# Scans, a sum of squares and the squares of heads in three mixers, put behind what the next product waits for

## The chip, the cores and the metric

The kernel runs on one core of a Trainium2 chip. The metric is the device time of one execution in microseconds (us), lower is better. Before the change the median of three runs is 1278.88 us (1277.93 to 1278.93).

## The reference, cut to what matters

Four transformer layers in a row work on one sequence of 256 rows of width 1024, all in float32. Each layer is a mixer and a gated feed-forward net. The mixers are: (1) dilated attention beside a state-space model; (2) a gated linear recurrence (RG-LRU); (3) latent attention (MLA) of 8 heads beside attention over 256 memory rows of 4 heads; (4) grouped-query attention of 8 heads on 2 key heads beside memory attention. The change touches mixers 2, 3 and 4.

```python
# mixer 2, after two gates r and i of the convolved input xc
a = exp(-8 * gate_r * softplus(-lam))
h[t] = a[t] * h[t-1] + sqrt(1 - a[t]**2) * gate_i[t] * xc[t]   # a scan along the rows
y = (h * gelu(z_right)) @ w_out                                # needs h of 1024 channels
# mixers 3 and 4, for each head of 128 channels
q = rmsnorm(q) * gain ; k = rmsnorm(k) * gain                  # mean of squares over the head
p = softmax(q @ k.T * scale) ; out = p @ v
```

## The kernel before, in words

**Products.** The rows lie in two tiles of 128. A weight matrix comes in chunks of 128 x 2048 floats (1 MB) by DMA into three RAW buffers (`weights`, L2473; SP waits for VectorE to be done with a buffer). For precision each chunk is split in a high part WH, by a copy on ScalarE (L1059, some 1.9 us), and a rest WL, by a subtraction on VectorE (L1655, some 2.3 us); activations are split in the same way (YAh by ScalarE, YAl by VectorE). Every product is then three matmuls: high by high, high by rest and rest by high (L451 to L453). `feed(c)` on ScalarE and on VectorE (L1061, L1657) splits the chunk three places after c, when its buffer is free. Transposes are matmuls by an identity matrix (L457).

**Order.** There is no planner: for each of the five engines one function issues a list of instructions written out by hand, and semaphores tie the lists together. Each engine works its own list strictly in order, so an instruction that waits holds all behind it. `fill` functions put other work between the steps of an attention, by head number h.

**Mixer 2.** The 1024 channels are eight tiles, worked as four pairs n = 0 to 3 ("heads" here). VectorE's `gates_scan` (L2095) multiplies (L2101) and scans (L2103) a pair, `gates_out` (L2105) multiplies by the gelu branch GT, ScalarE's `gates_out` (L1428) copies it to YAh, and VectorE's `gates_lo` (L2112) makes YAl (L1671). The product with w_out (`wide_mm`, L532, called with od_out) waits before each of its four chunks for the YAl of one pair (`out_ready`, L892). Ahead of it TensorE multiplies od2 and od3, whose results make GT; behind the first chunk it transposes the last half of them.

**Mixers 3 and 4.** `attention_ahead` exists for TensorE (L714), ScalarE (L1517) and VectorE (L2213). On TensorE a step h is: products of head h+2 (L723; waits for the exponentials of head h), transposes of the exponentials of head h, fill(h), pv of head h-1 (L747; waits for VectorE's copy of that head's transposes). ScalarE: exponentials of head h (L1523; wait for the maximum), fill(h). VectorE: maximum `top` of head h+2 (L2216), copy of the transposes of head h (L2238), fill(h).

Within these steps the last heads are still normalised. In mixer 3 query heads n1 (in PSUM banks 6 and 7) and key heads nk1 (banks 4 and 5) are squared by ScalarE into ZD and ZA, summed by `head_sum` (L1789, instruction L1792) on VectorE, turned to 1/sqrt by two small instructions on GpSimd (`rsqrt`, L2346: L2348 and L2350), scaled out of PSUM by `scaled_out` (L2203, instruction L2208), transposed by TensorE's `gain_turn` (L771) into banks 4 and 5, and copied with their gain by ScalarE's `gain_turn` (L1191, called qt1 and kt1 at h = 3 and 5 of L1530). `pvfree2` (L983) lets the first pv go only when n1 has left banks 6 and 7. The transposes of n1 (L979) wait for the scaled_out of nk1, since they write its banks.

In mixer 4 the memory queries g3 go the same way: ScalarE squares them head by head in `fill3` (L1629) with `head_squares` (L1174, instruction L1095, eight squares that each also give their sum), GpSimd makes the factors, VectorE scales them in its fill at h = 3 (`scaled`, L1782, instruction L1787), TensorE transposes them at h = 4 (L1036). `all_squares` (L1183, instruction L1185) is the other form, used elsewhere: one square over all 1024 elements and no sums, with a `head_sum` on VectorE behind it.

Of the kernel before, what the change touches and what calls it, by code (L numbers as in the profile page):

```python
# [198 lines left out]
def numbered(names):  # L199

    return {n: i + 1 for i, n in enumerate(names.split())}
# [11 lines left out]
class Tally:  # L213
# [5 lines left out]
    def up(self):  # L219
# [15 lines left out]
    zq pe zk mem1 n0 nk0 zm qp memk1 n1 nk1 row5 row6 g0 g2 g1 g3 row7"""  # L235
RSTD = numbered(NAMED_RSTD)
HSQ = counted(("memk0", 1), ("zq", 2), ("pe", 2), ("zk", 2), ("n0", 1), ("nk0", 1), ("zm", 1), ("qp", 1), ("memk1", 1),
              ("n1", 1), ("nk1", 1), ("g0", 8), ("g2", 4), ("g1", 8), ("g3", 8))
NZ = counted(*((n, 2) for n in "memk0 zq kp zk n0 nk0 zm qp memk1 n1 nk1 g0 g2 g1 g3".split()))
ZEV = counted(*((n, 2) for n in "za zb zc vt0 z2 vt1 g0 g2 g1 g3".split()))  # L240
GT = counted(("memk0", 2), ("qt0", 2), ("kt0", 2), ("qmt", 2), ("qpt", 2), ("memk1", 2), ("qt1", 2), ("kt1", 2),
             ("g0", 2), ("g2", 1), ("g1", 2), ("g3", 2))
HSUM = numbered("memk0 n0 nk0 zm qp memk1 n1 nk1")
SO = dict(memk0=8, zq=20, zk=22, zm=26, pe=24, memk1=8, qp=42, n0=34, nk0=8, n1=34, nk1=8, g3=26, g2=20, g0=8, g1=34)


def program(nc, A, PLAN, NCH):
# [10 lines left out]
    with top:  # L258
# [137 lines left out]
        JK2 = JK[:, :].rearrange("p (a b) -> p a b", a=2)  # L396
# [52 lines left out]
        def pe(e):  # L449
# [525 lines left out]
                    e.wait_ge(S.gout, GT["kt1"] + 2)  # L975

            def fill2(h):
                if h == 2:
                    gain_turn(ZD, "n1", (4, 5), lambda jp: e.wait_ge(S.nz, NZ["nk1"] + 2))  # L979
                elif h == 4:  # L980
                    gain_turn(ZA, "nk1", (4, 5), lambda jp: e.wait_ge(S.gout, GT["qt1"] + jp + 1))
# [73 lines left out]
        def act(e):  # L1055
# [37 lines left out]
            def squares(out, src, n, total):  # L1093

                return e.activation(out, src, ACT.Square, scale=n ** -0.5, accum_out=total)  # L1095

            def row_squares(ed):
                for t in range(2):
                    if t:
                        e.wait_ge(S.rowsq, 2 * ed + 1)  # L1100
                    squares(JK[:, :], X[:, t, :], 1024, st[:, 2 + t:3 + t]).then_inc(S.rowsq, 1)

            def post_squares(ed, t):
# [403 lines left out]
            def head_norm(name, src, nh=4, d=128, z=None):  # L1507
                e.wait_ge(S.z, ZEV[z] + 2)
                head_squares(name, src, nh, d)
# [119 lines left out]
            def fill3(h):  # L1629
                if h == 1:  # L1630
                    z_evac("g3", PLAN["gqa3"][1], (4, 5), Zg[3], scaled=True)
                elif h == 2:
                    gain_turn("g1", lambda j: QTg[:, 4 + j:6 + j, :], gqg[:, 1:2], (4, 5))
                    e.wait_ge(S.hsq, HSQ["g1"] + 8)
                    head_norm("g3", two(Zg[3]), 4, 128, "g3")
                elif h == 5:
                    gain_turn("g3", lambda j: QMg[:, j:j + 2, :], gqg[:, 0:1], (4, 5))
                elif h == 7:
                    feed(PLAN["gqa3"][1])
# [10 lines left out]
        def dve(e):  # L1650
# [138 lines left out]
            def head_sum(name, sq, d):  # L1789
                n = 1024 // d  # L1790
                e.wait_ge(S.hsq, HSQ[name] + 1)
                e.tensor_reduce(st[:, SO[name]:SO[name] + n], sq.rearrange("p a (h d) -> p (a h) d", d=d), AX.X, ADD).then_inc(S.hsum, 1)  # L1792
# [302 lines left out]
            def gates_scan(ns):  # L2095
                flat = lambda a, hs: a[:, hs, :].rearrange("p a b -> p (a b)")
                for n in ns:
                    hs = slice(2 * n, 2 * n + 2)
                    e.wait_ge(S.b3, n // 2 + 1)
                    e.wait_ge(S.b4, n // 2 + 1)  # L2100
                    e.tensor_tensor(TI[:, hs, :], TI[:, hs, :], HS[:, hs, :], MUL).then_inc(S.dv, dv.up())  # L2101
                    e.wait_ge(S.dv, dv.n)
                    e.tensor_tensor_scan(flat(HS, hs), flat(TR, hs), flat(TI, hs), 0.0, MUL, ADD).then_inc(S.dv, dv.up())  # L2103
# [8 lines left out]
            def gates_lo(ns):  # L2112
                for n in ns:
                    hs = slice(2 * n, 2 * n + 2)
                    e.wait_ge(S.b9, n + 1)
                    rest(YAl[:, hs, :], HS[:, hs, :], YAh[:, hs, :]).then_inc(S.b10, 1)
# [30 lines left out]
            feed(PLAN["od2"][0])  # L2147
            gates_scan((0, 1))
            feed(PLAN["od2"][1])
            gates_scan((2, 3))  # L2150
            gates_out((0, 1))
            gates_lo((0, 1))
            feed(PLAN["od3"][0])
            feed(PLAN["od3"][1])
            wide_mm(PLAN["od_out"], 3, last_heads)
# [132 lines left out]

            def fill2(h):
                if h == 0:  # L2290
                    head_sum("nk1", ZA[:, :, :], 128)
                    scaled_out("n1", ZD, (6, 7))
                elif h == 1:
                    scaled_out("nk1", ZA, (4, 5))
                    feed(PLAN["mem11"][1])
                elif h == 3:
                    feed(PLAN["qb1"][0])
                elif h == 7:
                    feed(PLAN["kvb1"][0])
# [30 lines left out]
            def fill3(h):  # L2330
                if h == 0:
                    feed(PLAN["gqa1"][1])
                elif h == 1:
                    feed(PLAN["gqa3"][0])
                elif h == 3:
                    scaled("g3", two(Zg[3]), 4, 128)
                elif h == 7:
                    feed(PLAN["gqa3"][1])
# [210 lines left out]
```

## Time and profile before

| | us |
|---|---|
| median of three runs (lowest, highest) | 1278.88 (1277.93, 1278.93) |
| the profiled execution's own time | 1277.36 |
| its span, first to last instruction | 1275.6 |
| TensorE busy (share) | 1247.0 (98%) |
| VectorE busy | 815.3 (64%) |
| ScalarE busy | 669.7 (52%) |
| GpSimd busy | 91.3 (7%) |
| weights read | 214.5 MB, 169 GB/s over the span |
| granted TensorE clock, mean | 0.998 |

"Busy" of TensorE counts matmuls whose ends are modelled, so that they overlap a little; gaps between them are what is to be read. PE is TensorE, DVE VectorE, ACT ScalarE, POOL GpSimd. In the views in order of time, a row gives start, duration, engine, line, instruction, output<-input with its size, how many of them are merged, and in brackets how long the engine stood idle before it and who released it.

### The profile page before, as it was taken

The page shows a single profiled execution, that of the slowest core. Times are in us where ns is not written, and L with a number is a line of the kernel's source. Part 1 is how long each engine was busy: PE and PEld are TensorE (multiplying, and loading weights), DVE is VectorE, ACT ScalarE, POOL GpSimd, SP SyncE. Part 2 cuts the span into 40 slices and gives each one's busy share as a digit, 9 for nine tenths or more (in the row PEclk, how much of TensorE's full clock was granted, in tenths as well). Part 3 has the DMA queues.
Part 4 walks back from the last instruction along what each step waited for, and adds up shares of the span by engine and source line. Part 5 has one row for each costly group of instructions (what it writes and reads, how often), then busy time and mean ns, then how long its engine had stood idle before and what let it go on. Part 6 is the DMA issues. An engine that isn't in the chain of part 4 may idle for free.

```text
span 1275.6 us, 15785 instructions
## 1 busy us (share of the span) xinstructions
PE 1247.0 (98%) x6366; PEld 1031.6 (81%) x6366; DVE 815.3 (64%) x1048; ACT 669.7 (52%) x975; POOL 91.3 (7%) x113
## 2 busy tenths in 40 slices
PE   6999999999999999999999999999999999999998
PEld 4877888888887888888888888888888888888886
DVE  7986766654787765564687656565546784665552
ACT  7666544433788554443587635444336653544431
POOL 2410100000110000000123100000000300000000
PEclk9999999999999999999999999999999999999999
DMA  7224465545644565545555224555455323555551
GB/s 298 100 84 143 171 212 184 193 171 198 215 165 165 182 208 188 192 172 198 171 198 192 73 75 161 212 180 198 166 197 177 132 100 132 198 178 185 195 173 62
DMA packets 32392, 216.60 MB, mean 170 GB/s; under 512 B 3888, under 2 KB 4272, under 8 KB 7232
## 3 DMA queue, kind: packets, MB, share of 16 engines
q1 hardware_dynamic: 30240, 210.19, 47.7%
q0 software_dynamic: 1360, 4.78, 1.2%
q8 instruction: 50, 0.82, 0.2%
q10 hardware_dynamic: 720, 0.63, 0.1%
q14 instruction: 22, 0.18, 0.0%
HBM read 214.54 MB, written 1.05 MB: 169 GB/s over the span
## 4 chain that ended last, share of the span: by engine, by line
PE 81%; DVE 10%; ACT 5%; issue 3%; DMA 1%; POOL 1%; SPq 0%; DVEq 0%; ACTq 0%
PE PS L451 22%; PE PS L453 22%; PE PS L452 22%; PE PS L457 4%; DVE WL L1655 3%; PE PS L488 2%; PE PS L491 2%; PE PS L489 2%; PE PS L723 2%; ACT WH L1059 2%; PE PS L747 1%; ACT HTh L1076 1%; DVE YG L1932 1%; DMA RAW<-in_w 1%; DVE st L1792 0%
## 5 line engine op out<-in xcount | busy, mean ns | idle before, releaser
L1655 DVE TENSOR_TENSOR WL<-RAW,WH 128x2048 fp32r<-128x2048 f32 (+2 forms) x200 | 443.9, 2222 | 327.9 <-ACT WH L1059 327.8
L1059 ACT ACTIVATE WH<-RAW 128x2048 fp32r<-128x2048 f32 (+2 forms) x200 | 371.7, 1862 | 381.1 <-PE PS L453 380.1
L451 PE MATMUL PS<-WH,HTh 128*128 128x512 f32 (+1 forms) x848 | 335.0, 395 | 1.9 <-DVE WL L1655 1.9
L453 PE MATMUL PS<-WH,HTl 128*128 128x512 f32 (+1 forms) x848 | 329.0, 388 | 0.0
L452 PE MATMUL PS<-WL,HTh 128*128 128x512 f32 (+1 forms) x848 | 328.4, 387 | 0.0
L451 PEld LDWEIGHTS PS<-WH,HTh 128*128 128x128 f32 x848 | 159.5, 188 | 34.4 <-DVE WL L1655 3.2
L453 PEld LDWEIGHTS PS<-WH,HTl 128*128 128x128 f32 x848 | 159.2, 188 | 33.3
L452 PEld LDWEIGHTS PS<-WL,HTh 128*128 128x128 f32 x848 | 159.6, 188 | 30.5
L451 PE MATMUL PS<-WH,YAh 128*128 128x512 f32 x402 | 158.9, 395 | 2.6 <-DVE YAl L1671 2.2
L453 PE MATMUL PS<-WH,YAl 128*128 128x512 f32 x402 | 156.7, 390 | 0.0
L452 PE MATMUL PS<-WL,YAh 128*128 128x512 f32 x402 | 156.5, 389 | 0.0
L451 PEld LDWEIGHTS PS<-WH,YAh 128*128 128x128 f32 x402 | 75.5, 188 | 18.7 <-issue 4.0
L453 PEld LDWEIGHTS PS<-WH,YAl 128*128 128x128 f32 x402 | 75.4, 188 | 15.9
L452 PEld LDWEIGHTS PS<-WL,YAh 128*128 128x128 f32 x402 | 75.6, 188 | 14.9
L2348 POOL TENSOR_SCALAR st<-st 128x2 f32<-128x2 f32 (+4 forms) x33 | 19.1, 579 | 762.9 <-ACT JK L1095 692.2
L488 PE MATMUL PS<-WH,HTh 128*128 128x512 f32 (+1 forms) x128 | 52.8, 412 | 3.9 <-DVE WL L1655 2.6
L1076 ACT ACTIVATE HTh<-PS,cst 128x128 fp32r<-128x128 f32 (+1 forms) x136 | 39.2, 379 | 26.8 <-PE PS L457 26.8
L491 PE MATMUL PS<-WH,HTl 128*128 128x512 f32 (+1 forms) x128 | 50.5, 395 | 0.0
L489 PE MATMUL PS<-WL,HTh 128*128 128x512 f32 (+1 forms) x128 | 50.5, 394 | 0.0
L1672 DVE SCALAR_TENSOR_TENSOR HTl<-PS,cst,HTh 128x128 fp32r<-128x128 f32 (+1 forms) x136 | 38.9, 351 | 12.5 <-ACT HTh L1076 12.0
L2350 POOL TENSOR_TENSOR st<-st,mh 128x2 f32<-128x2 f32 (+4 forms) x33 | 39.6, 1199 | 2.8
L1076 ACT ACTIVATE YAh<-PS 128x512 fp32r<-128x512 f32 x38 | 21.6, 583 | 25.6 <-PE PS L457 25.6
(364 smaller groups left out, 1488.8 us busy)
## 6 DMA issues: line engine op xcount, KB each, us to landing
RAW<-in_w SPq DMA_DIRECT2D x196, 1024.0 KB, 4.9
BC<-in_rows POOLq DMA_DIRECT2D x4, 512.0 KB, 3.9
YG<-in_mem POOLq DMA_DIRECT2D x4, 512.0 KB, 4.8
X<-in_x SPq DMA_DIRECT2D x2, 512.0 KB, 6.4
RAW<-in_w SPq DMA_DIRECT2D x4, 256.0 KB, 5.8
BC<-in_s SPq DMA_DIRECT2D x1, 512.0 KB, 11.0
BB<-in_s SPq DMA_DIRECT2D x1, 512.0 KB, 11.5
YG<-in_s SPq DMA_DIRECT2D x1, 512.0 KB, 12.3
```

The source lines that it names most:

```text
L451: e.matmul(out, ah, bh, start=start, stop=False)
L452: e.matmul(out, ah, bl, start=False, stop=False)
L453: return e.matmul(out, al, bh, start=False, stop=stop)
L457: return e.transpose(out, src, ident[0:p, 0:p])
L488: e.matmul(out, HTh[:, k, ts], WH[:, c % NW, w], start=k == 0, stop=False)
L489: e.matmul(out, HTh[:, k, ts], WL[:, c % NW, w], start=False, stop=False)
L491: return e.matmul(out, HTl[:, k, ts], WH[:, c % NW, w], start=False, stop=k == 7)
L1059: e.activation(WH[:, c % NW, w], RAW[:, c % NR, w], ACT.Copy).then_inc(S.hi, 1)
L1076: return e.activation(out, src, ACT.Copy, scale=scale)
L1655: e.tensor_tensor(WL[:, c % NW, w], RAW[:, c % NR, w], WH[:, c % NW, w].bitcast(f32), SUB).then_inc(S.lo, 1)
L1672: return e.scalar_tensor_tensor(out, src, gain, hi.bitcast(f32), MUL, SUB)
L2350: e.tensor_tensor(st[:, at:at + n], st[:, at:at + n], mh[:, 0:n], ALU.pow).then_inc(S.rs, 1)
```

## The change

Mixer 2: on VectorE the scans of pairs 2 and 3 come after the gates of pairs 0 and 1 and their YAl. Mixer 3: on VectorE head_sum of nk1 moves from head step 0 to 1, scaled_out of nk1 from step 1 to 2, so that the split of a chunk (`feed(PLAN["mem11"][1])`) now comes before it; on TensorE the transposes of n1 move from step 2 to 3. Mixer 4: the eight squares of g3 with sums become one square without sums, and VectorE sums them in its step 2; the counts of two semaphores follow. ScalarE's last row squares, which write the same scratch, wait for that sum.

```diff
-              ("n1", 1), ("nk1", 1), ("g0", 8), ("g2", 4), ("g1", 8), ("g3", 8))
+              ("n1", 1), ("nk1", 1), ("g0", 8), ("g2", 4), ("g1", 8), ("g3", 1))
...
-HSUM = numbered("memk0 n0 nk0 zm qp memk1 n1 nk1")
+HSUM = numbered("memk0 n0 nk0 zm qp memk1 n1 nk1 g3")
...
 # TensorE
             def fill2(h):
-                if h == 2:
+                if h == 3:
                     gain_turn(ZD, "n1", (4, 5), lambda jp: e.wait_ge(S.nz, NZ["nk1"] + 2))
...
 # ScalarE
                     if t:
                         e.wait_ge(S.rowsq, 2 * ed + 1)
+                    elif ed == 7:
+                        e.wait_ge(S.hsum, HSUM["g3"])
...
                     e.wait_ge(S.hsq, HSQ["g1"] + 8)
-                    head_norm("g3", two(Zg[3]), 4, 128, "g3")
+                    e.wait_ge(S.z, ZEV["g3"] + 2)
+                    all_squares(JK2, Zg[3][:, :, :], 128)
...
 # VectorE
             feed(PLAN["od2"][1])
-            gates_scan((2, 3))
             gates_out((0, 1))
             gates_lo((0, 1))
+            gates_scan((2, 3))
             feed(PLAN["od3"][0])
...
             def fill2(h):
                 if h == 0:
-                    head_sum("nk1", ZA[:, :, :], 128)
                     scaled_out("n1", ZD, (6, 7))
                 elif h == 1:
+                    head_sum("nk1", ZA[:, :, :], 128)
+                    feed(PLAN["mem11"][1])
+                elif h == 2:
                     scaled_out("nk1", ZA, (4, 5))
-                    feed(PLAN["mem11"][1])
...
                     feed(PLAN["gqa3"][0])
+                elif h == 2:
+                    head_sum("g3", JK2, 128)
                 elif h == 3:
```

## Rows read from the trace of the kernel before

**Rows 1.** The page's first part: busy us, share of the span, instructions

```profile
PE 1247.0 (98%) x6366; PEld 1031.6 (81%) x6366; DVE 815.3 (64%) x1048; ACT 669.7 (52%) x975; POOL 91.3 (7%) x113
```

**Rows 2.** Waits of PE over the whole span: total us, times, longest us

```profile
PE PS L451 <- DVE YAl L1671: 2.2, 2, 1.2
...
PE PS L747 <- DVE Z L2208: 1.2, 1, 1.2
```

**Rows 3.** PE in order of time, start of the product with od_out

```profile
413.23 0.47 PE L451 MATMUL PS<-WH,YAh 128*128 128x512 f32 x1 [1.18 <-DVE YAl L1671]
...
418.79 1.04 PE L457 MATMUL PS<-ident,ZN 128*128 128x128 f32 x8
```

**Rows 4.** DVE in order of time, end of mixer 2

```profile
407.18 0.69 DVE L2101 TENSOR_TENSOR TI<-TI,XC 128x512 f32<-128x512 f32 x1
...
411.01 1.29 DVE L2110 TENSOR_TENSOR XC<-XC,GT 128x512 f32<-128x512 f32 x2
412.39 1.29 DVE L1671 TENSOR_TENSOR YAl<-XC,YAh 128x512 fp32r<-128x512 f32 x2
```

**Rows 5.** ACT in order of time, the same stretch

```profile
406.71 1.92 ACT L1059 ACTIVATE WH<-RAW 128x2048 fp32r<-128x2048 f32 x1 [0.93 <-PE PS L453]
```

**Rows 6.** PE in order of time, attention of mixer 3

```profile
716.71 1.13 PE L747 MATMUL PS<-YG,Z 128*128 128x128 f32 x8 [1.19 <-DVE Z L2208]
...
718.54 1.56 PE L457 MATMUL PS<-ident,Z 128*128 128x128 f32 x12
719.94 1.06 PE L747 MATMUL PS<-YG,Z 128*128 128x128 f32 x8
720.83 1.03 PE L723 MATMUL PS<-KM,QMT 128*128 128x256 f32 x4
...
723.40 1.03 PE L723 MATMUL PS<-KM,QMT 128*128 128x256 f32 x4
```

**Rows 7.** DVE in order of time, attention of mixer 3

```profile
712.95 0.69 DVE L2216 TENSOR_REDUCE A2M<-PS 128x2 f32<-128x512 f32 x1 [1.03 <-PE PS L723]
...
714.16 1.21 DVE L1792 TENSOR_REDUCE st<-Z 128x8 f32<-128x1024 f32 x1
...
717.68 1.28 DVE L2208 TENSOR_TENSOR Z<-PS,st 128x512 f32<-128x512 f32 x2
718.87 2.28 DVE L1655 TENSOR_TENSOR WL<-RAW,WH 128x2048 fp32r<-128x2048 f32 x1
```

**Rows 8.** ACT in order of time, the two copies of qt1 in mixer 3

```profile
719.70 1.27 ACT L1076 ACTIVATE QTn<-PS,gq 128x512 f32<-128x512 f32 x2 [1.49 <-PE PS L457]
```

**Rows 9.** A DVE split and POOL, in order of time, before and in the attention

```profile
690.30 2.28 DVE L1655 TENSOR_TENSOR WL<-RAW,WH 128x2048 fp32r<-128x2048 f32 x1
...
690.47 2.21 POOL L2348 TENSOR_SCALAR st<-st 128x8 f32<-128x8 f32 x1 [8.86 <-DVE st L1792]
...
715.46 0.24 POOL L2348 TENSOR_SCALAR st<-st 128x8 f32<-128x8 f32 x1 [8.78 <-DVE st L1792]
715.78 1.67 POOL L2350 TENSOR_TENSOR st<-st,mh 128x8 f32<-128x8 f32 x1
```

**Rows 10.** PE in order of time, attention of mixer 4

```profile
1025.98 1.13 PE L723 MATMUL PS<-KTg,QTg 128*128 128x256 f32 x4 [0.91 <-ACT A3P L1523]
...
1030.52 1.06 PE L747 MATMUL PS<-Zg,A3PT 128*128 128x128 f32 x8
```

**Rows 11.** DVE in order of time, attention of mixer 4

```profile
1026.52 0.68 DVE L2238 COPY A3PT<-PS 128x512 f32<-128x512 f32 x1
...
1028.36 1.28 DVE L1787 TENSOR_TENSOR Zg<-Zg,st 128x512 f32<-128x512 f32 x2
```

**Rows 12.** ACT in order of time: first square of g3, and the next exponential

```profile
1022.45 0.31 ACT L1095 ACTIVATE JK<-Zg 128x128 f32<-128x128 f32 x1
...
1024.93 0.45 ACT L1523 ACTIVATE A3P<-PS,A3M 128x256 f32<-128x256 f32 x1
```

**Rows 13.** The square over 1024 elements, by its line: ns min/median/max

```profile
L1185 ACT ACTIVATE JK<-Z x3: 1061/1063/1063, 668.5 to 686.5; 128x1024 f32<-128x1024 f32 x3
```

## The prediction

> **What bounds the kernel now.** I read the page first: TensorE is busy for 98% of the span [rows 1]. What doesn't take TensorE off the path cannot shorten anything, and whatever makes it wait 1 us costs 1 us, since long stretches of weight products behind it have no slack to give back. Then the waits of TensorE, to see how much is there to win: in the three mixers that the diff touches there is one wait each, about 1.2 us for the recurrent mixer (of the 2.2 us in two waits for YAl), 1.2 us for Z in the second mixer and 0.9 us for A3P in the fourth [rows 2, 10]. All three together are 3.3 us, or 0.26%. Less than 0.2% (2.6 us) is what a measurement of this kernel can hardly tell from no change. So the question is only how many of the three go, and whether the work that was moved comes back as a new wait. For that I read the three stretches engine by engine, in order of time.
>
> **Recurrent mixer (gates_scan, L2148 to L2152).** TensorE ends its last od3 product and stands idle for 1.18 us until 413.23, waiting for the first YAl [rows 3]. VectorE before it: multiplication and scan of heads 2 and 3 from 407.18 to 411.01, which is 3.83 us, then the gates of heads 0 and 1, with the first YAl at 412.39 [rows 4]. The output product needs only heads 0 and 1 at its start. With the scans behind gates_lo, the gates start at 407.2. ScalarE is then in a weight split until 406.71 + 1.92 = 408.6 [rows 5], and its two copies of this size take 1.27 us [rows 8], so the first one is ready at 409.3 and the first YAl at 410.0, the second at 410.6. TensorE comes at about 412: no wait. The idle time goes by the record as 1.18; as the end of a pipelined matmul is modelled, the pause is a little longer, and I take 1.3 us (0.9 to 1.5). What is late next: the scans of heads 2 and 3 run from 410.6 to 414.4, and behind them the split for the second chunk of od_out until 416.7 (2.3 us, as [rows 7] has such a split). TensorE wants that chunk after its first chunk and the transposes, which lie 5.56 us behind the start [rows 3]: 412.0 + 5.6 + 0.8 = 418.4. 1.7 us to spare; if that cover were gone, each us would cost one. The transfer that SP starts into the RAW buffer freed by this split goes out 0.8 us later; it fills a buffer needed three chunks on, so I cost it at nothing. **-1.3 us.**
>
> **Second mixer, VectorE.** Before: top and copy of head 0 from 712.95, head_sum nk1 at 714.16, scaled_out n1, top and copy of head 1, scaled_out nk1 at 717.68, then the 2.28 us split from 718.87 [rows 7]. It is one unbroken row of work. TensorE's first pv waits for scaled_out n1 and starts at 716.71 after 1.19 us of idle [rows 6]. With head_sum (1.13 us with its start-up overlapped) behind it, this pv starts at 715.6: 1.13 us won for the moment.
>
> But scaled_out nk1 now stands behind head_sum nk1, the split of 2.2 us, and top and copy of head 2 (1.21 us, as those of head 0). Laid end to end: head_sum from 716.55 to 717.76, split 717.68 to 719.96, top and copy to 721.1. GpSimd must turn the sum into a factor between them. Its first instruction takes 0.24 us and the power 1.67 us when VectorE reads PSUM beside it, but 2.21 us when VectorE has begun a weight split just before it: the split of 690.30 ends at 692.58, the GpSimd instruction at 692.68 [rows 9]. The new order makes exactly that sequence, head_sum and then a split. So: GpSimd until 720.05, power until 721.8, scaled_out nk1 from 721.83 to 723.1.
>
> The Trainium skill (SBUF — State Buffer, Who interferes with whom) says that a VectorE instruction with two SBUF inputs and a GpSimd instruction that reads SBUF exclude each other for a whole instruction, whoever starts first. By that rule the wait is certain and not a matter of luck, and the trace agrees in its 2.21 us against 0.24 us; without it the sum of this mixer would be 0.75 us less.
>
> **Second mixer, who waits for it.** The diff moves the turn of n1 on TensorE from head 2 to head 3, and there it still waits for scaled_out nk1, because it writes the banks that this reads. Before it started at 718.54 + 4 x 0.108 = 719.0 (12 transposes take 1.30 us, up to 719.84) and met a result that was just there [rows 6]. Now TensorE has done pv 0, products 4, transposes 2, pv 1, products 5 and transposes 3 by about 720.0, and waits until 723.2. Then 8 transposes, 0.87 us, and pv 2, 0.89 us (719.94 to 720.83): 724.95 where products 6 stood at 723.40 before [rows 6], so +1.55 us. And ScalarE works in order: behind its exponentials of head 3 it waits for that turn to copy qt1, and the exponentials of head 4 are queued behind the copies. The copies began 0.73 us after the turn's start and take 1.27 us together [rows 8]; from an exponential pair's start to the product that it frees is 1.05 us (1024.93 to 1025.98, [rows 10, 12]). 723.2 + 0.73 + 1.16 + 1.05 = 726.1. Against 723.40: **+2.7 us**, and from there on TensorE has no gap in this attention to win it back. If GpSimd isn't held it is +1.9, if ScalarE's queue costs nothing either +0.8; if the split and one more group lie in the way, +3.5.
>
> **Fourth mixer.** ScalarE's eight squares with their reads of the sum take 2.48 us (1022.45 to 1024.93, [rows 12]) in front of the exponentials that products 5 wait for until 1025.98, 0.91 us idle [rows 10]. One square over 1024 elements is 1.06 us [rows 13]: exponentials at 1023.5, products 5 at 1024.9, 1.1 us sooner. pv 2, two steps on, needs VectorE's copy of head 2, which runs from 1026.52 to 1027.2 [rows 11] behind two splits that nothing moved. So pv 2 starts as before, and the gain is gone by then. And the sums must now be made: head_sum of 1.21 us on VectorE at 1027.12, to 1028.33; top and copy of head 3 until 1029.5; GpSimd 0.24 + 1.67 and 0.2 of hand-over, VectorE's neighbours being readers of PSUM: 1030.4. Scaling of g3, 1.28 us as one pair from 1028.36 to 1029.64 before [rows 11], runs from 1030.4 to 1031.7. The turn of g3 on TensorE waits for both halves: 7 more transposes, and pv 3 at 1032.5 instead of 1030.52 [rows 10]. **+2.0 us** (from +1.5 to +2.8, if GpSimd is held once). The wait that ScalarE gets before the last row squares (hsum) is over 60 us old by then: nothing. No DMA is issued by what moves, and POOL's queue only waits for another signal.
>
> **The sum.** -1.3 + 2.7 + 2.0 = +3.4 us. The profiled execution took 1277.36 us, its span being 1275.6, so 1280.8 for its like. The median of the three runs is 1278.88, 1.5 above it; on that I put the forecast: **1282.3 us**, slower by 0.27%.
>
> **Rivals.** (1) *The change does what its title says*: the three waits go and no new one comes, -3.3 to -3.7 us, about 1275.4. For it: the freed instructions are indeed the ones waited for. Against: TensorE's turn of n1 is tied to scaled_out nk1, and that stands over 4 us later on VectorE; it needs turn and copy to find it done at 720.0, and the order written out by hand excludes it. It decides if VectorE starts scaled_out nk1 before 719. I give it 0.07. (2) *The turns cost less*: GpSimd slips in before the split, or ScalarE's copies don't hold products 6, or the fourth mixer's chain is shorter; +1.0 to +2.5 us, 1279.9 to 1281.4, within 0.2%. 0.22. (3) *The work comes back in the recurrent mixer too*: od_out's second chunk or heads 2 and 3 are late, the 1.3 us are not won: about +4.7, 1283.6. Against it stand the 1.7 us to spare. 0.09. The forecast itself, +2.6 to +4.2: 0.62.
>
> **How the numbers follow.** Faster by over 0.2%: only rival 1, 0.07. Within 0.2%: rival 2 and a little of the forecast's low end, 0.25. Slower: 0.68. The range from 1279.8 to 1284.2 takes in the forecast with the bounds of its terms (-1.5 + 1.9 + 1.5 = +1.9 up to -0.9 + 3.5 + 2.8 = +5.4) and most of rivals 2 and 3; it leaves out rival 1 and the ends at which all terms err one way.
>
> **What would show it.** Right: no idle of TensorE for YAl near 412; the first pv of the second mixer about 1.1 us sooner after its transposes; then an idle of about 3 us before the transposes of n1, released by Z of scaled_out, a GpSimd instruction of about 2.2 us beside the split, and 1 us before products 6, released by ScalarE; in the fourth mixer an idle of about 1.7 us before the transposes of g3, released by the scaling. Wrong: if the transposes of n1 wait for less than 1.5 us, or VectorE has idle time between head_sum and that split, or the pv 2 of the fourth mixer starts 1 us sooner and stays ahead.

## The result and the profile after

The changed kernel takes 1283.51 us as the median of six runs (1282.06 to 1284.24); six runs of the kernel before, in the same series, have a median of 1277.99 (1277.38 to 1278.93). The ratio is 1.0041 with a 95% interval of 1.0028 to 1.0054: slower by 5.5 us between the medians; the interval is 3.6 to 6.9 us. The forecast was 1282.3 us, slower, in a range from 1279.8 to 1284.2. Times in this part come from the records; "shifted" means that a fixed offset between two traces has been taken off. What the prediction calls the second mixer is mixer 3 of the sections ahead of it, its fourth mixer is mixer 4.

The profiled execution took 1282.89 us with a span of 1281.1 and a mean granted clock of 0.996 (before: 1277.36, 1275.6 and 0.998). Part 1 of its page, against [rows 1], has two surprises for a reader who looks at totals: ScalarE does 2.4 us less and VectorE only 0.6 us more, and yet the kernel is slower. TensorE has 2.6 us more of busy time with the same number of instructions; most of that is clock, not work, and comes back below.

```profile
PE 1249.6 (98%) x6366; PEld 1033.5 (81%) x6366; DVE 815.9 (64%) x1049; ACT 667.3 (52%) x960; POOL 91.1 (7%) x113
```

The waits of TensorE over the whole span (total us, times, longest us) say where it went. Of the two waits for YAl in [rows 2] one is left, and it lies outside the changed stretches; the 1.2 us for Z at L747 is gone. New are 3.0 us for Z, 1.7 us for Zg, 0.9 us for ScalarE's Z and 0.9 us for A3PT.

```profile
PE PS L457 <- DVE Z L2211: 3.0, 1, 3.0
...
PE PS L457 <- DVE Zg L1790: 1.7, 2, 1.5
...
PE PS L451 <- DVE YAl L1674: 1.1, 1, 1.1
PE PS L723 <- ACT Z L1525: 0.9, 1, 0.9
PE PS L747 <- DVE A3PT L2241: 0.9, 1, 0.9
```

**Mixer 2.** TensorE in order of time around the start of the product with od_out, against [rows 3]: the last matmul of od3, then the first one with YAh, with no idle time between them. The transposes of the last heads follow 5.45 us after that start.

```profile
412.20 0.39 PE L453 MATMUL PS<-WH,HTl 128*128 128x512 f32 x1
412.42 0.39 PE L451 MATMUL PS<-WH,YAh 128*128 128x512 f32 x1
...
417.87 1.04 PE L457 MATMUL PS<-ident,ZN 128*128 128x128 f32 x8
```

VectorE in the same stretch, against [rows 4]: gates, the two YAl, then the scans, then the splits. YAl begins 2.7 us earlier than before (409.71 against 412.39), and TensorE, which comes at 412.42, is now the later of the two.

```profile
407.70 1.29 DVE L2113 TENSOR_TENSOR XC<-XC,GT 128x512 f32<-128x512 f32 x2
409.71 1.29 DVE L1674 TENSOR_TENSOR YAl<-XC,YAh 128x512 fp32r<-128x512 f32 x2 [0.73 <-ACT YAh L1076]
410.93 0.68 DVE L2104 TENSOR_TENSOR TI<-TI,XC 128x512 f32<-128x512 f32 x1
...
414.63 4.47 DVE L1658 TENSOR_TENSOR WL<-RAW,WH 128x2048 fp32r<-128x2048 f32 x2
```

**Mixer 3.** This trace runs 0.99 us ahead of the other when the attention begins (its first products start at 705.20 against 706.19). TensorE, against [rows 6]: pv 0 starts without a wait; behind the transposes of head 3 it stands for 2.97 us before the 8 transposes of n1, and for 0.94 us before products 6.

```profile
714.59 1.13 PE L747 MATMUL PS<-YG,Z 128*128 128x128 f32 x8
...
718.62 0.60 PE L457 MATMUL PS<-ident,Z 128*128 128x128 f32 x4
722.19 1.09 PE L457 MATMUL PS<-ident,Z 128*128 128x128 f32 x8 [2.97 <-DVE Z L2211]
723.12 1.06 PE L747 MATMUL PS<-YG,Z 128*128 128x128 f32 x8
725.11 1.13 PE L723 MATMUL PS<-KM,QMT 128*128 128x256 f32 x4 [0.94 <-ACT Z L1525]
```

VectorE and then GpSimd, against [rows 7] and [rows 9]: head_sum, the split begun behind it, and scaled_out of nk1. GpSimd's small instruction begins at 716.85, inside the split that began at 716.68, and ends with it: 2.21 us instead of 0.24. So VectorE itself waits, 0.68 us, for the factor.

```profile
715.56 1.21 DVE L1795 TENSOR_REDUCE st<-Z 128x8 f32<-128x1024 f32 x1
716.68 2.28 DVE L1658 TENSOR_TENSOR WL<-RAW,WH 128x2048 fp32r<-128x2048 f32 x1
...
720.84 1.29 DVE L2211 TENSOR_TENSOR Z<-PS,st 128x512 f32<-128x512 f32 x2 [0.68 <-POOL st L2356]
```

```profile
716.85 2.21 POOL L2354 TENSOR_SCALAR st<-st 128x8 f32<-128x8 f32 x1 [11.18 <-DVE st L1795]
719.14 1.67 POOL L2356 TENSOR_TENSOR st<-st,mh 128x8 f32<-128x8 f32 x1
```

ScalarE, against [rows 8]: the copies of qt1 waited 6.46 us for the transposes, and the exponentials of head 4, for which products 6 wait, stand behind them.

```profile
722.88 1.26 ACT L1076 ACTIVATE QTn<-PS,gq 128x512 f32<-128x512 f32 x2 [6.46 <-PE PS L457]
724.03 0.47 ACT L1525 ACTIVATE Z<-PS,A2M 128x256 f32<-128x256 f32 x1
```

**Mixer 4.** Here this trace is 1.80 us behind (first products at 1015.35 against 1013.55). TensorE, against [rows 10]: products 5 no longer wait (1026.71, shifted 1024.91, so 1.07 us sooner), pv 2 then waits 0.88 us for VectorE's copy (1029.06, shifted 1027.26, against 1027.39 before), and the transposes of g3 wait 1.47 and 0.28 us for the scaling.

```profile
1026.71 1.03 PE L723 MATMUL PS<-KTg,QTg 128*128 128x256 f32 x4
...
1029.06 1.16 PE L747 MATMUL PS<-Zg,A3PT 128*128 128x128 f32 x8 [0.88 <-DVE A3PT L2241]
...
1032.99 0.33 PE L457 MATMUL PS<-ident,Zg 128*128 128x128 f32 x1 [1.47 <-DVE Zg L1790]
1033.59 1.02 PE L457 MATMUL PS<-ident,Zg 128*128 128x128 f32 x7 [0.28 <-DVE Zg L1790]
1034.41 1.91 PE L747 MATMUL PS<-Zg,A3PT 128*128 128x128 f32 x8
1036.12 1.87 PE L723 MATMUL PS<-KTg,QTg 128*128 128x256 f32 x4
```

VectorE and GpSimd, against [rows 11]: sum at 1028.92, factor from 1030.22, scaling at 1032.24, 3.32 us behind the start of the sum. Beside readers of PSUM GpSimd's first instruction takes 0.24 us, as it did before in mixer 3 [rows 9].

```profile
1028.92 1.21 DVE L1795 TENSOR_REDUCE st<-JK 128x8 f32<-128x1024 f32 x1
...
1032.24 1.29 DVE L1790 TENSOR_TENSOR Zg<-Zg,st 128x512 f32<-128x512 f32 x2 [0.92 <-POOL st L2356]
```

```profile
1030.22 0.24 POOL L2354 TENSOR_SCALAR st<-st 128x8 f32<-128x8 f32 x1 [16.77 <-DVE st L1795]
1030.54 1.67 POOL L2356 TENSOR_TENSOR st<-st,mh 128x8 f32<-128x8 f32 x1
```

The last two TensorE rows hold something else. The same pv of 8 matmuls took 1.06 us in [rows 10], and the products 1.13; here they take 1.91 and 1.87. The view by stretches of 5 us (length; busy us and count of PE, PEld, DVE, ACT and POOL; granted clock; DMA share; GB/s) gives the reason: behind the idle time the granted clock fell to half, 1.2 instead of 2.4 GHz, for a part of this stretch, in which TensorE is busy all the time.

```profile
1035.00:1040.00 5.00, 5.00 (x31) 4.53 (x30) 2.57 (x4) 1.56 (x6) 0.00 (x0) 0.72 0.01 3
```

**Where the time went.** Measured from the first product of each attention to the first matmul of the output product behind it, mixer 3 takes 43.35 us (before 40.55) and mixer 4 39.32 us (before 35.57); between the two it is 266.8 us in both. At the start of od_out the trace is 0.54 us behind by its last od3 matmul (412.20 against 411.66) and 0.81 us ahead by the first matmul of od_out (412.42 against 413.23): 1.35 us won. The 0.54 us was lost in the first 40 us of the program, where nothing was changed, at a granted clock of 0.66 from 30 to 40 us against 0.83. So +0.5 - 1.35 - 0.2 + 2.80 + 3.75 = +5.5 us, of which the waits explain 2.80 in mixer 3 and, as the next section shows, 2.10 in mixer 4. The other 1.65 us of mixer 4 are clock. In this pair of traces nothing is left over, but the next section shows that other pairs divide the loss differently.

### The profile page after: what moved, and what is told of

It reads as the page before. It is cut to its first block, busy times and chain, and to the rows that moved or that the text cites. A ratio compares the mean times of both kernels' runs of the same rounds, so it can differ in the third digit from the quotient of the medians.

```text
span 1281.1 us, 15771 instructions
## 1 busy us (share of the span) xinstructions
PE 1249.6 (98%) x6366; PEld 1033.5 (81%) x6366; DVE 815.9 (64%) x1049; ACT 667.3 (52%) x960; POOL 91.1 (7%) x113
## 4 chain that ended last, share of the span: by engine, by line
PE 85%; DVE 7%; ACT 4%; issue 1%; POOL 1%; DMA 1%; SPq 0%; DVEq 0%; ACTq 0%
PE PS L451 24%; PE PS L453 24%; PE PS L452 24%; PE PS L457 5%; DVE WL L1658 2%; PE PS L488 2%; PE PS L491 2%; PE PS L489 2%; PE PS L723 2%; ACT WH L1059 1%; PE PS L747 1%; ACT HTh L1076 1%; DMA RAW<-in_w 1%; POOL st L2354 1%; DVE st L1795 1%
```

## The experiments

Every kernel was timed beside runs of the kernel before on the same chip, except for two single executions (before_look, after_look). Three series were made; each gives its own median of the kernel before (1278.14 of 33 runs, 1278.01 of 12, 1277.92 of 9). "Attention of mixer 3" and "of mixer 4" are the stretches just defined.

**Each part alone.** Three kernels, each with one of the three edits and otherwise the kernel before.

```diff
# od_only: VectorE, mixer 2
             feed(PLAN["od2"][1])
-            gates_scan((2, 3))
             gates_out((0, 1))
             gates_lo((0, 1))
+            gates_scan((2, 3))
```

> Only the scans of pairs 2 and 3 are moved behind the gates and YAl of pairs 0 and 1. Theory (the wait for YAl goes and nothing takes its place): no idle of TensorE before the product with od_out, 1.3 us shorter. Rival (the parts are coupled, and this part's gain shows only in the profile): no change, within 0.5 us.

Measured: 1276.44 us (1275.57 to 1277.74, 11 runs), ratio 0.9986 (0.9978 to 0.9995), which is -1.7 us. In its trace the only wait of TensorE between 380 and 440 us is one of 0.2 us for HTh, and the first matmul of od_out follows the last of od3 by 0.23 us. The scans cost TensorE nothing behind the gates. This part does what the title says.

```diff
# mla_only: TensorE and VectorE, mixer 3
-                if h == 2:
+                if h == 3:
                     gain_turn(ZD, "n1", (4, 5), ...
...
                 if h == 0:
-                    head_sum("nk1", ZA[:, :, :], 128)
                     scaled_out("n1", ZD, (6, 7))
                 elif h == 1:
-                    scaled_out("nk1", ZA, (4, 5))
+                    head_sum("nk1", ZA[:, :, :], 128)
                     feed(PLAN["mem11"][1])
+                elif h == 2:
+                    scaled_out("nk1", ZA, (4, 5))
```

> Only the changes of mixer 3. Theory (scaled_out of nk1 comes too late for the transposes of n1, and ScalarE's copies hold the exponentials of head 4): 2.8 us longer, an idle of 3.0 us before the transposes and 0.9 us before the products of head 6, clock at 1.00. Rival (the loss needs the shifted start or a lowered TensorE clock): under 1 us longer.

Measured: 1280.89 us (1280.04 to 1282.26, 11 runs), ratio 1.0020 (1.0012 to 1.0029), +2.75 us. The attention of mixer 3 takes 43.35 us, +2.80, to the hundredth what it takes in the whole change. Its waits of TensorE from 700 to 760 us are the same two:

```profile
PE PS L457 <- DVE Z L2208: 3.0, 1, 3.0
PE PS L723 <- ACT Z L1523: 0.9, 1, 0.9
```

```diff
# gqa_only: ScalarE and VectorE, mixer 4 (with the two counts)
-                    head_norm("g3", two(Zg[3]), 4, 128, "g3")
+                    e.wait_ge(S.z, ZEV["g3"] + 2)
+                    all_squares(JK2, Zg[3][:, :, :], 128)
...
+                elif h == 2:
+                    head_sum("g3", JK2, 128)
```

> Only the changes of mixer 4. Theory A (waits alone): 2.0 us longer. Theory B (the idle time of TensorE in this attention makes the granted clock fall for some us right after it, as the profile after the change shows it at 0.72 in the stretch 1035 to 1040): 3.7 us longer, matmuls behind the transposes of g3 at twice their time for about 2 to 3 us. Rival C (the fall of the clock was one of that execution and comes at random): 2.0 us in most runs, a wider spread.

Measured: 1280.73 us (1279.65 to 1282.48, 11 runs), ratio 1.0021 (1.0012 to 1.0030), +2.6 us. The attention of mixer 4 takes 37.67 us, +2.10, with the waits of the whole change (1.7 for Zg, 0.9 for A3PT). But the pv behind the transposes of g3 runs at full clock, unlike in the whole change, and this is the whole difference between 37.67 and 39.32. The expectation that this part alone brings the fall along (its theory B, 3.7 us) did not come true:

```profile
1033.75 0.98 PE L457 MATMUL PS<-ident,Zg 128*128 128x128 f32 x7 [0.27 <-DVE Zg L1790]
1034.57 1.06 PE L747 MATMUL PS<-Zg,A3PT 128*128 128x128 f32 x8
```

By these stretches the three parts make -1.35 + 2.80 + 2.10 = +3.55 us, by the medians -1.7 + 2.75 + 2.6 = +3.65, where the whole change has +5.5, and +5.3 when repeated below. The intervals of the single ratios are about 1 us wide to either side, so the medians alone would not prove that something is missing; the clock rows show it.

**The whole change again (after_again), and one more execution of each kernel (after_look, before_look).** No edit.

> The changed kernel again, beside the others of this series. The three parts alone gave -1.7, +2.8 and +2.6 us by medians, together +3.7. Theory (the granted TensorE clock falls to 1.2 GHz for some us in the first 120 us of every execution and in some executions once more in the attention of mixer 4 behind its idle time; the rest adds up): executions fall in two groups some 1.7 us apart, the lowest near 4.4 us above the lowest of before, the median +4.5 to +5.5. Rival (the waits of mixers 3 and 4 strengthen each other): a single group at +5.5 with little spread.

> The changed kernel, one more look. By the waits the attention of mixer 3 takes 43.35 us and that of mixer 4 37.67 us; a fall of the clock in one of them adds about 1.7 us to it. Theory: one of the two has it in some executions. Rival: lengths as by the waits, always.

> The kernel before, one more look at where the granted clock falls. Theory: below 1.00 only in the first 120 us (and at the very end); none in the attentions of mixers 3 and 4. Rival: as often there as in the changed kernel. Stage lengths: 40.55 us for the attention of mixer 3 and 35.57 us for that of mixer 4 again.

Measured: after_again 1283.32 us (1282.55 to 1284.11, 5 runs), ratio 1.0042 (1.0029 to 1.0054). At +5.3 us the result repeats. The two groups of executions that were expected can't be seen: the five lie within 1.6 us, and the lowest is 5.5 us above the lowest of the kernel before, not 4.4. Its trace has the same waits in both attentions, at 43.36 and 37.67 us, and no fall of the clock in either; the one fall besides that of the program's start came about 108 us into the span. So this execution, 5.2 us longer than the one profiled before the change (1282.55 against 1277.36), owes 3.55 us to the waits and the other 1.6 us to stretches that the change doesn't touch: its first product of mixer 3 starts at 706.48, which is 0.3 us later than in the kernel before where it should be 1.35 us earlier. after_look took 1281.45 us: the clock fell in mixer 3, behind the wait for Z (44.09 us, in which the wait for ScalarE is swallowed), and mixer 4 took 37.66. before_look took 1279.08 us, with both attentions as before (40.55 and 35.58) and a fall at 108 us. So the stretches repeat to 0.01 us wherever no fall lies in them, and the falls of the clock don't repeat: their place changes from one execution to the next. In the three profiles of the whole change they cost 1.65, 0.74 and 0 us in the two attentions, 0.8 us on average.

Each run also has its mean granted clock, to the third decimal. Averaged over the runs, with the kernels that are described further down:

```
kernel         runs   mean clock
at most one of the two new idle stretches (mixer 3, mixer 4):
before           33     0.9975   (in the two later series 0.9978 of 12, 0.9973 of 9)
od_only          11     0.9980
mla_only         11     0.9973
gqa_only         11     0.9973
best_1           11     0.9974
best_2            5     0.9976
both:
changed (first)   6     0.9960
changed (again)   5     0.9958
early_sum         6     0.9963
copies_later      7     0.9961
half_split        5     0.9956
gqa_longer        5     0.9956
```

0.9975 - 0.9959 = 0.0016 of 1281 us are 2.0 us at full clock that were not granted (2.6 us for the second series against its own 0.9978). The loss of time is at most that, since clock missing while TensorE stands idle costs nothing. It is the size of what is missing, 5.4 - 3.65 = 1.75 us. The 34 runs of kernels with both new idle stretches and the 49 with one or none, each kernel by its mean, do not overlap. And the loss looks to be in most executions, not in a few: the lowest of all timed runs of the kernel before plus 3.55 us of waits would be 1280.5 us, and the eleven timed runs of the changed kernel begin at 1282.06.

**The sum of nk1 earlier** (early_sum): the changed kernel, with the sum put in front of the attention, where VectorE waits for TensorE anyway.

```diff
             head_sum("n1", ZD[:, :, :], 128)
+            head_sum("nk1", ZA[:, :, :], 128)
...
                 elif h == 1:
-                    head_sum("nk1", ZA[:, :, :], 128)
                     feed(PLAN["mem11"][1])
```

> The changed kernel, but with the head_sum of nk1 ahead of the attention of mixer 3, so that neither it nor GpSimd lies between the weight split and scaled_out. Theory (of the 2.7 us of mixer 3, head_sum's 1.1 us and GpSimd's hold of 0.7 us on VectorE's path cost about 1.9, the split the rest): 1.9 us shorter than the changed kernel, an idle of about 1.2 us before the transposes of n1. Rival (the split alone makes it late): under 0.8 us shorter.

Measured: 1281.83 us (1279.64 to 1282.49, 6 runs), ratio 1.0026 (1.0015 to 1.0038), 1.5 us less than after_again in the same series. The attention of mixer 3 takes 41.45 us, 1.90 less. GpSimd's first instruction, at 707.80, takes 0.24 us, the idle time before the transposes of n1 falls from 2.97 to 1.07 us, and the wait for ScalarE stays:

```profile
721.69 1.09 PE L457 MATMUL PS<-ident,Z 128*128 128x128 f32 x8 [1.07 <-DVE Z L2211]
722.61 1.06 PE L747 MATMUL PS<-YG,Z 128*128 128x128 f32 x8
724.61 1.13 PE L723 MATMUL PS<-KM,QMT 128*128 128x256 f32 x4 [0.94 <-ACT Z L1525]
```

So 1.9 us of the 2.97 come from the sum standing in that place and from GpSimd held behind it; the rest is put down to the split itself, which still stands before scaled_out. By the medians the gain is 1.5 us; this profile has a fall of the clock in mixer 4 (39.32 us).

**ScalarE's copies of qt1 one step later** (copies_later): the changed kernel, so that the exponentials of head 4 pass them.

```diff
-                elif h == 3:
+                elif h == 4:
                     gain_turn("qt1", ...
```

> The changed kernel, but ScalarE's two copies of qt1 stand behind the exponentials of head 4, not before them. Theory (ScalarE's exponentials of head 4 are queued behind copies that wait for TensorE): the 0.9 us of idle before the products of head 6 goes, 1.1 us shorter than the changed kernel. Rival (VectorE's maxima are late anyway): no change.

Measured: 1280.69 us (1280.15 to 1284.35, 7 runs), ratio 1.0027 (1.0016 to 1.0038), 2.6 us below after_again by the medians and 1.7 by the means, 1281.47 against 1283.21: five runs lie within 1.0 us, two at 1283.03 and 1284.35. The wait for ScalarE is gone from the trace, as it should be if its queue is the cause. The gain in the medians is more than the 0.94 us of that wait (1.1 us was expected). The rest isn't explained; the granted clock moves with it, 0.997 in each of the five and 0.994 in the two. The profiled execution itself has a fall of the clock right behind the wait for Z, which gives the 0.94 us back: the attention takes 43.54 us. TensorE:

```profile
721.19 1.97 PE L457 MATMUL PS<-ident,Z 128*128 128x128 f32 x8 [2.98 <-DVE Z L2211]
722.95 1.60 PE L747 MATMUL PS<-YG,Z 128*128 128x128 f32 x8
724.39 1.03 PE L723 MATMUL PS<-KM,QMT 128*128 128x256 f32 x4
```

1.97 and 1.60 us stand where 1.09 and 1.06 stood, and the clock of that stretch (720 to 725 us) is 0.66.

**The split in two halves** (half_split): the changed kernel; the chunk between the sum and scaled_out is subtracted in two instructions of 1024 columns.

```diff
+                e.tensor_tensor(WL[:, n % NW, 0:1024], RAW[:, n % NR, 0:1024], WH[:, n % NW, 0:1024].bitcast(f32), SUB)
+                split_lo(n, slice(1024, CH))
...
-                    feed(PLAN["mem11"][1])
+                    feed_halves(PLAN["mem11"][1])
```

> The changed kernel, but the weight split behind head_sum nk1 is made in two halves of 1024 columns. Theory A (GpSimd's first instruction is held for the length of one VectorE instruction): it takes about 1.2 us and not 2.2; the power then runs beside or holds up the second half; scaled_out nk1 up to 0.7 us sooner, 0.5 to 0.8 us shorter than the changed kernel. Rival B (it is held until VectorE has no such instruction at hand): 2.2 us as before, no gain. Rival C (the power goes first and holds the second half for its 1.67 us): GpSimd early, but VectorE 1 us later, about 0.4 us longer.

Measured: 1282.83 us (1281.13 to 1284.31, 5 runs), ratio 1.0039 (1.0025 to 1.0053), 0.5 us under after_again, less than this can tell from nothing. VectorE's halves and GpSimd's two instructions:

```profile
717.83 1.21 DVE L1675 TENSOR_TENSOR WL<-RAW,WH 128x1024 fp32r<-128x1024 f32 x1
718.96 1.22 DVE L1658 TENSOR_TENSOR WL<-RAW,WH 128x1024 fp32r<-128x1024 f32 x1
...
721.74 1.29 DVE L2219 TENSOR_TENSOR Z<-PS,st 128x512 f32<-128x512 f32 x2 [0.36 <-POOL st L2364]
```

```profile
718.00 1.14 POOL L2362 TENSOR_SCALAR st<-st 128x8 f32<-128x8 f32 x1 [11.19 <-DVE st L1803]
719.23 2.48 POOL L2364 TENSOR_TENSOR st<-st,mh 128x8 f32<-128x8 f32 x1
```

The first GpSimd instruction is held for one half (1.14 us, up to 719.14, where 2.21 us had been up to the end of the whole split), and then the power is held for the second half: 2.48 us instead of 1.67. Together 3.7 us instead of 4.0, and TensorE's idle time falls from 2.97 to 2.72. That is theory A of the expectation, and it excludes B (2.2 us again) and C (the power first), but the gain by the trace is 0.25 us and not 0.5 to 0.8, since the second hold was not in it. The hold goes by the VectorE instruction, and each GpSimd instruction meets it anew. The Trainium skill (SBUF — State Buffer, Who interferes with whom) has this as a rule, the shared pair of ports being taken for a whole instruction; the trace agrees in all three lengths, 2.21, 1.14 and 0.24 us. This profile, too, has a fall of the clock behind the idle time (8 transposes in 1.97 us), and 43.83 us for the attention.

**The sum of g3 later** (gqa_longer): the changed kernel, with the idle time before the transposes of g3 made longer.

```diff
-                elif h == 2:
-                    head_sum("g3", JK2, 128)
                 elif h == 3:
+                    head_sum("g3", JK2, 128)
                     scaled("g3", two(Zg[3]), 4, 128)
```

> The changed kernel, but head_sum of g3 stands in VectorE's step 3, right before the scaling, not in step 2. By the waits alone: pv 2 of mixer 4 starts sooner, scaled g3 and with it the transposes 1.2 us later, so 0.9 to 1.2 us longer than the changed kernel. Theory (idle time of TensorE makes the granted clock fall in this attention): more executions fall, mean clock lower, 1.2 to 2.8 us longer. Rival (the falls have nothing to do with it): 0.9 to 1.2 us longer and the clock as in the changed kernel.

Measured: 1284.79 us (1283.85 to 1285.51, 5 runs), ratio 1.0049 (1.0035 to 1.0063), 1.5 us over after_again, which was timed in another series (+6.9 against +5.3 by the kernel before of each); the waits for Zg are 1.2 us longer (2.9 against 1.7), so nearly all of it is the wait. The mean clock, 0.9956 against 0.9958, is no lower, so the longer idle time did not bring more falls, as the theory had it; and pv 2 waits 0.88 us as before, though it was expected sooner. The attention of mixer 4 takes 40.51 us, which is 37.67 + 1.2 and another 1.65 for a fall of the clock:

```profile
1035.44 0.33 PE L457 MATMUL PS<-ident,Zg 128*128 128x128 f32 x1 [2.66 <-DVE Zg L1790]
...
1037.19 1.92 PE L747 MATMUL PS<-Zg,A3PT 128*128 128x128 f32 x8
```

The 1.65 us is the same as in the changed kernel's first profile and in that of early_sum (39.32 us each). In these three executions a fall in mixer 4 costs the same behind the shorter and the longer idle time.

**A better order** (best_1 and best_2), from the kernel before. Mixer 2 as changed. In mixer 3 only the sum of nk1 goes ahead of the attention; the turn stays at head 2 and scaled_out at step 1. In mixer 4 the one square, with the sum on VectorE in step 1, in place of a weight split that goes to step 5; best_2 also moves the next split from step 7 to 11.

```diff
             head_sum("n1", ZD[:, :, :], 128)
+            head_sum("nk1", ZA[:, :, :], 128)
...
                 if h == 0:
-                    head_sum("nk1", ZA[:, :, :], 128)
                     scaled_out("n1", ZD, (6, 7))
...
                 elif h == 1:
-                    feed(PLAN["gqa3"][0])
+                    head_sum("g3", JK2, 128)
                 elif h == 3:
                     scaled("g3", two(Zg[3]), 4, 128)
+                elif h == 5:
+                    feed(PLAN["gqa3"][0])
-                elif h == 7:
+                elif h == 11:          # best_2 alone
                     feed(PLAN["gqa3"][1])
```

> The part of mixer 2 as in the change; in mixer 3 the order of before, but with the head_sum of nk1 ahead of the attention, where VectorE idled for 3.5 us; in mixer 4 one square over g3, its head_sum in VectorE's step 1 in place of a weight split, and that split in step 5, where VectorE idled for 1.5 us. Theory (all three waits go if nothing that TensorE needs stands behind the added sum): 1.3 + 1.2 + 1.1 = 3.6 us shorter, 1274.4. Rival (the late split of mixer 4 delays the later heads): the gain of mixer 4 is lost, 2.5 us shorter.

> best_1, with the second weight split of mixer 4 moved from VectorE's step 7 to 11. In best_1 TensorE still waited 0.6 us for a copy behind these two splits. Theory: that idle goes and with the split also the smaller stops behind it, 0.6 to 0.9 us shorter than best_1, 1274.3. Rival (the first chunks of the product that follows are late now): no gain, an idle for a weight split in the product with out1.

Measured: best_1 1275.07 us (1273.95 to 1276.85, 11 runs), ratio 0.9975 (0.9966 to 0.9984), -3.1 us; attentions 39.42 and 35.12 us, with 0.6 us for A3PT as the longest wait left in mixer 4. That is 1.13 us won in mixer 3, as expected, but 0.45 us of the expected 1.1 in mixer 4. best_2 1273.94 us (1272.52 to 1274.87, 5 runs), ratio 0.9965 (0.9953 to 0.9978), -4.0 us; attentions 39.42 and 33.78 us. Best_2 is faster than both kernels of this case. The view of the waits lists none of TensorE in either attention of its trace. VectorE's sum and scaling in mixer 4, and between them GpSimd's first instruction:

```profile
1020.65 1.21 DVE L1795 TENSOR_REDUCE st<-JK 128x8 f32<-128x1024 f32 x1
...
1024.16 1.28 DVE L1790 TENSOR_TENSOR Zg<-Zg,st 128x512 f32<-128x512 f32 x2
```

```profile
1021.94 0.24 POOL L2353 TENSOR_SCALAR st<-st 128x8 f32<-128x8 f32 x1 [13.37 <-DVE st L1795]
```

The sum stands one step earlier, no split follows it, and the scaling finds its factor ready: no idle time stands before it. Two splits were moved out of the way as well, so the 1.8 us that best_2 wins in mixer 4 (33.78 against 35.57) are not the gain of the sum's place alone.

## Why the prediction was right, and where it was short

**The direction and each wait.** Slower was right, and for the reasons given. Point by point, with the offset of the traces taken off:

- *Mixer 2, -1.3 us*: -1.35 by the profile, -1.7 (-2.8 to -0.6) by the timed kernel with this part alone. The transposes were to begin 5.6 us after the start (5.45 measured), and the second chunk behind them found its split done, with no wait.
- *Mixer 3, +2.7 us*: +2.80. pv 0 was forecast for 715.6 and came at 715.58; scaled_out of nk1 for 721.83, and came at 721.83; the transposes of n1 for 723.2 (723.18); products 6 for 726.1 (726.10). early_sum and copies_later take its two halves apart: 1.90 us for the sum in its place, 0.94 us for ScalarE's queue. That GpSimd's 2.21 us is a hold by VectorE's instruction is confirmed by half_split.
- *Mixer 4, +2.0 us*: +2.10. Products 5 came 1.07 us sooner (1.1 said), pv 2 as before but for 0.13 us, pv 3 at 1032.61 (1032.5 said).

**The step that fell short** is "The sum". It says: -1.3 + 2.7 + 2.0 = +3.4 us. The waits make +3.55, and the change made +5.5 and +5.3 by the medians of two series, and +5.5 between the two profiled executions. The step treats TensorE's idle time as costing its own length and no more. It had no term for the granted clock, although "What bounds the kernel now" starts from TensorE's busy share and the granted clock is in the same page. The +5.5 us lie just above the +5.4 that the bounds of its own terms reach. What the runs show in its place: of the seven profiles that have both new idle stretches (after, after_again, after_look, copies_later, half_split, gqa_longer, and early_sum, whose first one is only 1.07 us) six have the clock fall to 1.2 GHz right behind one of them. Of the seven that have one of them or neither, none falls in an attention of mixers 3 or 4. One fall costs 1.65 us in mixer 4 (39.32 against 37.67), in mixer 3 0.74 (44.09 against 43.35), since the wait for ScalarE that lay behind it disappears in it. The mean clock of the timed runs bears that out: 0.9956 to 0.9963 in the kernels with both, 0.9973 to 0.9980 in the others.

What isn't settled: why an execution falls in one place and not in the other, and why mla_only, with 3.0 us of idle time, kept its clock (0.9973 over 11 runs) where the whole change did not. Each part alone was profiled once; that it takes both rests on the mean clocks above, which don't tell where a fall lies. That the falls make up the whole of the missing 1.75 us is argued from the mean clock, not shown by a run in which only the clock differed: the three profiles of the whole change have 0.8 us of it on average in the two attentions, and in one of them (after_again) the rest over the waits lies at 108 us, ahead of everything that was changed.

**The forecast of the time** lies nearer (1282.3 against 1283.51) than that of the difference (+3.4 against +5.5). The median of three runs on which it was built, 1278.88, is 0.9 us above that of the six in which those three are contained, 1277.99; that error took away nearly half of the other, 2.1 us. This is luck: on 1277.99 the same sum gives 1281.4 us.

**The rivals.** (1) The three waits go and none comes: excluded, as argued, by the order of VectorE's list. best_1 and best_2 show that it was to be had, by -3.1 and -4.0 us, once the sum of nk1 stood where VectorE has nothing to do and the sum of g3 stood a step earlier, with the splits moved out of its way. (2) The turns cost less: no; GpSimd was held, and ScalarE's copies did hold products 6. (3) The recurrent mixer loses its gain: no, see od_only. A total of +4.7 us, its number, would have been nearer to the measured one for a wrong reason. None of the three had the clock.

## What to carry to other kernels

Before work is moved away from what the next product waits for, look on the same engine's list at what it is moved behind, and follow its result to every reader: here 1.2 us of work was moved behind a 2.3 us split, the small GpSimd step between them was held by that split, and two engines had the late result at the head of their queues. The place for such work is where its engine is idle already: the sum of nk1 ahead of the attention cost nothing and gave the 1.1 us that the move was meant for. Where there is no such place, something else has to make room, as a split did for the sum of g3. And where TensorE is nearly always busy, several new waits of the size seen here (1.5 to 3 us) should be costed with the clock that may fall behind them: 0.7 to 1.7 us for each fall in an attention here, some 1.75 us over the timed runs.

## What the runs showed of the hardware

- The granted clock can fall to 1.2 GHz in the middle of a kernel whose TensorE is busy for 98% of the span. In the attentions that happened behind an idle time of 2.72 to 2.98 us (mixer 3) or behind 1.47 and 0.28 us together, with 0.88 us some 4 us earlier (mixer 4; 2.66 and 0.27 us in gqa_longer); the same idle times left the clock alone in other executions. A pv of 8 matmuls then takes 1.91 us for 1.06. The Trainium skill (TensorE: Matmul & The Clock Gate, What's actually happening) has two levels, chosen by how busy TensorE has been; the durations here agree with the two levels, and the granted clock is 0.50 in the changed kernel from 32 to 36 us.
- Halving VectorE's instruction splits GpSimd's hold and hardly shortens it: with the subtraction in two halves the two GpSimd instructions take 1.14 + 2.48 us, with it whole 2.21 + 1.67, beside readers of PSUM 0.24 + 1.67.
- Unchanged stretches have such falls as well: 13 of the 14 profiles have one in the first 40 us (0.83 as the mean from 30 to 40 us in the kernel before, 0.66 in the changed one, which was 0.5 us later from there on), and six of the 14 have one at about 108 us. A difference of 0.5 to 1.7 us between two single executions can be this. The early fall, too, stands behind an idle time, 2.91 to 2.96 us in all 14, in which TensorE waits for ScalarE's Qn; before_look, the one without it, does the same seven transposes in 0.98 us instead of 1.76:

```profile
31.23 0.33 PE L457 MATMUL PS<-ident,Qn 128*128 128x128 f32 x1 [2.92 <-ACT Qn L1076]
31.81 1.76 PE L457 MATMUL PS<-ident,Qn 128*128 128x128 f32 x7 [0.25 <-ACT Qn L1076]
```

```profile
31.98 0.98 PE L457 MATMUL PS<-ident,Qn 128*128 128x128 f32 x7 [0.25 <-ACT Qn L1076]
```

The first two lines are of the kernel before, the last is of before_look. So the trace of the kernel before already shows that its clock can fall behind an idle time of 3 us. The last microseconds of a profile, in which TensorE is done, are left out of these counts.
